# Gathering expert rows of two tables in alternation, and summing one of them wholly on the matrix engine

## The reference, cut to what matters

```python
def _peer(xn, wq, keys, u_tab, v_tab):
    q = (xt @ wq).reshape(t, PEER_HEADS, 2, PEER_HALF)
    sc = jnp.einsum('thkd,hknd->thkn', q, keys)
    s1, i1 = lax.top_k(sc[:, :, 0], 16); s2, i2 = lax.top_k(sc[:, :, 1], 16)
    ...                                   # best 16 of the 256 sums: experts, gates
    def block(args):                      # 128 tokens at a time
        ub = u_tab[eb]
        act = _gelu(jnp.einsum('td,thkd->thk', xb, ub)) * gb
        vb = v_tab[eb]
        return jnp.einsum('thk,thkd->td', act, vb)
```

## Time and profile before

| | |
|---|---|
| median of 3 runs | 3803.68 us (3803.42 to 3810.28) |
| profiled execution | 3807.15 us |
| its span, first to last instruction | 3805.4 us |
| busy: PE / DVE / POOL / ACT | 2685.4 / 2037.5 / 1864.6 / 802.3 us |
| granted PE clock, mean over the span | 0.850 |
| indirect transfers | 537 MB in 1024 rows |
| all transfers | 694 MB, mean 182 GB/s |

### The profile page before, as it was taken

How to read it: one execution, slowest core, us unless ns; L and a number is a source line. 1 busy time by engine, 2 the same in 40 slices (tenths; PEclk the granted TensorE clock), 3 DMA queues, 4 the chain that set the end, 5 groups by cost and what they waited for, 6 DMA issues and landing times.

```text
span 3805.4 us, 40545 instructions
## 1 busy us (share of the span) xinstructions
PE 2685.4 (71%) x15872; PEld 2087.4 (55%) x15872; DVE 2037.5 (54%) x4133; ACT 802.3 (21%) x1515; POOL 1864.6 (49%) x1389
## 2 busy tenths in 40 slices
PE   6521887207852287543767888888899998999999
PEld 4410444103431144211225777777789997789999
DVE  6589877888787878588444534454220103532010
ACT  2100111001110011111113322332332322433231
POOL 0166655775567756477752322221354543126463
PEclk7665998558986599766998988898899999999999
DMA  5398889997999879999981200000123332012332
GB/s 172 128 309 301 279 286 334 321 340 259 313 322 333 310 267 345 332 339 341 356 306 34 67 23 1 1 1 1 56 73 95 89 87 59 23 45 78 95 94 78
DMA packets 417984, 694.02 MB, mean 182 GB/s; under 512 B 35784, under 2 KB 280691, under 8 KB 417667
## 3 DMA queue, kind: packets, MB, share of 16 engines
q0 software_dynamic: 147456, 536.94, 39.7%
q1 hardware_dynamic: 270339, 154.50, 13.9%
HBM read 689.26 MB, written 2.10 MB: 182 GB/s over the span
## 4 chain that ended last, share of the span: by engine, by line
PE 51%; DVE 16%; POOL 13%; DMA 10%; issue 6%; ACT 3%; SPq 1%; DVEq 0%; ACTq 0%
PE PS L1593 25%; POOL ring L601 13%; DMA ring<-in_peer_v,eidx 7%; PE PS L768 6%; DMA ring<-in_peer_u,eidx 2%; PE PS L747 2%; DVE ring L1301 2%; PE PS L1495 1%; PE PS L1504 1%; PE PS L653 1%; PE PS L1501 1%; DVE X L1316 1%; PE PS L1603 1%; DVE W L1175 1%; PE PS L1615 1%
## 5 line engine op out<-in xcount | busy, mean ns | idle before, releaser
L601 POOL DMA_INDIRECT ring<-in_peer_u,eidx x512 | 635.8, 1242 | 404.0 <-DVE eidx L1278 177.9
L601 POOL DMA_INDIRECT ring<-in_peer_v,eidx x512 | 588.0, 1148 | 351.4 <-PE PS L768 192.1
L1593 PE MATMUL PS<-held_uH,GW 128*128 128x264 f32 (+1 forms) x3648 | 693.1, 290 | 35.9 <-POOL BIG_value L2120 31.8
L1301 DVE CUSTOM_DVE_ANT_0 ring<-ring,hn 128x1024 f32<-128x1024 f32 x512 | 614.7, 1223 | 115.6 <-DMA ring<-in_peer_u,eidx 106.8
L2106 POOL TENSOR_TENSOR GW<-held_wr,GW 128x1024 fp32r<-128x1024 f32 x178 | 428.6, 2409 | 453.2 <-ACT GW L1883 453.2
L768 PE MATMUL PS<-ring,dg 128*128 128x512 f32 x1024 | 528.2, 655 | 172.4 <-DMA ring<-in_peer_v,eidx 168.0
L1593 PEld LDWEIGHTS PS<-held_uH,GW 128*128 128x128 f32 x3648 | 581.7, 193 | 48.9 <-issue 32.4
L1593 PE MATMUL PS<-BIG_value,GW 128*128 128x264 f32 (+1 forms) x1824 | 486.1, 287 | 0.0
L768 PEld LDWEIGHTS PS<-ring,dg 128*128 128x128 f32 x1024 | 196.2, 206 | 460.6 <-DMA ring<-in_peer_v,eidx 276.6
L1316 DVE SCALAR_TENSOR_TENSOR X<-ring,gact,X 128x1024 f32<-128x1024 f32 x256 | 328.6, 1284 | 186.0 <-DMA ring<-in_peer_v,eidx 181.4
L1593 PE MATMUL PS<-hid,GW 128*128 128x264 f32 (+1 forms) x3072 | 370.4, 282 | 0.0
(11 more groups left out here) (465 smaller groups left out, 3613.2 us busy)
## 6 DMA issues: line engine op xcount, KB each, us to landing
held_wr<-in_w_ff SPq DMA_DIRECT2D x128, 512.0 KB, 4.0
wqr<-in_peer_wq SPq DMA_DIRECT2D x64, 512.0 KB
held_wr<-in_w_in_ab SPq DMA_DIRECT2D x18, 512.0 KB, 3.9
ring<-in_peer_u,eidx POOLq DMA_INDIRECT x512
ring<-in_peer_v,eidx POOLq DMA_INDIRECT x512
BIG<-in_w_in SPq DMA_DIRECT2D x4, 1536.0 KB, 11.4
held_wr<-in_w_qkv_c SPq DMA_DIRECT2D x12, 512.0 KB, 3.8
w_out<-in_w_out SPq DMA_DIRECT2D x1, 4096.0 KB, 19.0
```

Source lines behind the costliest of these rows:

```text
L601: e.indirect_dma_start(out=ring[:, i % RING, :], out_offset=None, in_=rows_u if k < HK else rows_v, in_offset=bass.IndirectOffsetOnAxis(ap ...
L1301: e.tensor_tensor_reduce(row, row, hn[:, :], 1.0, 0.0, ALU.mult, ALU.add, act[:, k:k + 1]).then_inc(*n.up(e_dot))
L1593: ins = e.matmul(bank[b + a][:, 0:w], w_[:, k * P:(k + 1) * P], x_[:, c0:c0 + w], start=(first and z in (0, 2)), stop=(last and z >= 4))
```

## The change

The new `first_order` keeps two counters, one of U rows and one of V rows. In block 0 the 128 U rows run as before, beside the front of block 0 only; then come 110 V rows of block 0 alone (HK - LAG), with all 76 steps of front 1 spread evenly over them. From then on each pass of the loop takes one U row of block 1, 2 or 3 and one V row, which lies 18 rows behind: V rows 110 to 127 of the block before, then 0 to 109 of the same block. In blocks 1 and 2 a step of the next front follows in two passes of three. In block 3 a step of the tails follows in one pass of four, until the first step of tail 2 is out. The last 18 V rows follow alone, then the end of block 3, and then what is left of the late steps: nine steps of tail 2, the projection for block 3, and tail 3.

All V rows go to PE; `expert_add` is gone, and every V row has a diagonal from ACT, up to three ahead. Gelu and the weighing are done for one head (16 columns) at a time. The ring has the same six slots, and its order follows the list.

```diff
+LAG = 18
...
-    def experts(blk, others, pace):
-        while heads(blk) < 1:
+    def add_u(others):
+        blk, k = divmod(count["u"], HK)
+        while heads(blk) < k // TOPK + 1:
             step(others)
-        order.append(("begin", blk))
-        if blk == NB - 1:
-            order.append(("second",))
-        for k in range(HK):
-            while heads(blk) < k // TOPK + 1:
-                step(others)
-            order.append(("u", blk, k))
-            if k % pace[0] == 0:
-                step(others)
-        while taken[("front", blk)] < FRONT_STEPS:
-            step(others)
-        order.append(("gate", blk))
-        for k in range(HK):
-            order.append(("v", blk, k))
-            if k % pace[1] == 0:
-                step(others)
-        order.append(("end", blk))
+        if k == 0:
+            order.append(("begin", blk))
+            if blk == NB - 1:
+                order.append(("second",))
+        order.append(("u", blk, k))
+        count["u"] += 1
+        if k % TOPK == TOPK - 1:
+            order.append(("gelu", blk, k // TOPK))
+        if ended:
+            order.append(("end", ended.pop()))
+    def add_v():
+        m = count["v"]
+        for x in range(m, min(m + NDG, NB * HK)):
+            blk, k = divmod(x, HK)
+            head = x // TOPK
+            if x in diagonals or count["u"] < TOPK * (head + 1) or taken[("front", blk)] < FRONT_STEPS:
+                continue
+            if head not in weighed:
+                order.append(("weigh", blk, k // TOPK))
+                weighed.add(head)
+            order.append(("dg", blk, k))
+            diagonals.add(x)
+        blk, k = divmod(m, HK)
+        order.append(("v", blk, k))
+        count["v"] += 1
+        if k == HK - 1:
+            ended.append(blk)
     fronts = [(("front", 0), FRONT_STEPS)]
     for _ in range(7):
...
-    while taken[("front", 0)] < 13:
+    for k in range(HK):
+        add_u(fronts)
+        if k % 3 == 0:
+            step(fronts)
+    while taken[("front", 0)] < FRONT_STEPS:
         step(fronts)
-    for blk, pace in ((0, (3, 2)), (1, (8, 2)), (2, (8, 2))):
-        fronts.append((("front", blk + 1), FRONT_STEPS))
-        experts(blk, fronts, pace)
-    while fronts:
-        step(fronts)
+    fronts.append((("front", 1), FRONT_STEPS))
+    for k in range(HK - LAG):
+        add_v()
+        while fronts and taken.get(("front", 1), 0) * (HK - LAG) < FRONT_STEPS * (k + 1):
+            step(fronts)
     late = []
     for b in range(3):
         late += [(("pproj", b), 1), (("tail", b), TAIL_STEPS)]
     late.append((("pproj", 3), 1))
-    experts(3, late, (4, 4))
+    for blk in range(1, NB):
+        for k in range(HK):
+            add_u(fronts)
+            if k == 0 and blk + 1 < NB:
+                fronts.append((("front", blk + 1), FRONT_STEPS))
+            add_v()
+            if blk == NB - 1:
+                if k % 4 == 3 and taken.get(("tail", 2), 0) < 1:
+                    step(late)
+            elif k % 3:
+                step(fronts)
+        while blk + 1 < NB and taken[("front", blk + 1)] < FRONT_STEPS:
+            step(fronts)
+    while count["v"] < NB * HK:
+        add_v()
+    order.append(("end", ended.pop()))
...
+    gathers = [name for name in first_order() if name[0] in ("u", "v")]
+    place = {name: i for i, name in enumerate(gathers)}
     def slot_free(e, i):
-        j = i - RING
-        if j < 0:
-            return
-        blk, k = j // 256, j % 256
-        if k < HK:
-            e.wait_ge(e_dot, HK * blk + k + 1)
-        elif k % 2:
-            e.wait_ge(e_pv, 64 * blk + (k - HK) // 2 + 1)
-        else:
-            e.wait_ge(e_ax, 64 * blk + (k - HK) // 2 + 1)
+        if i >= RING:
+            kind, blk, k = gathers[i - RING]
+            e.wait_ge(e_dot if kind == "u" else e_pv, HK * blk + k + 1)
     def first_pool(e):
-        for blk in range(NB):
-            for k in range(2 * HK):
-                i = 256 * blk + k
-                if k < HK and k % TOPK == 0:
-                    e.wait_ge(r_idx, NH * blk + k // TOPK + 1)
-                slot_free(e, i)
-                e.indirect_dma_start(
-                    out=ring[:, i % RING, :], out_offset=None, in_=rows_u if k < HK else rows_v,
-                    in_offset=bass.IndirectOffsetOnAxis(ap=eidx[:, blk % 2, k % HK:k % HK + 1], axis=0),
-                ).then_inc(d_r[i % RING], 16)
+        for i, (kind, blk, k) in enumerate(gathers):
+            if kind == "u" and k % TOPK == 0:
+                e.wait_ge(r_idx, NH * blk + k // TOPK + 1)
+            slot_free(e, i)
+            e.indirect_dma_start(
+                out=ring[:, i % RING, :], out_offset=None, in_=rows_u if kind == "u" else rows_v,
+                in_offset=bass.IndirectOffsetOnAxis(ap=eidx[:, blk % 2, k:k + 1], axis=0),
+            ).then_inc(d_r[i % RING], 16)
...
     def expert_sum(e, n, blk, k):
-        if k % 2:
-            i = k // 2
-            e.wait_ge(*row_there(256 * blk + HK + k))
-            e.wait_ge(e_dg, 64 * blk + i + 1)
-            for c in range(2):
-                ins = e.matmul(bank[6 + c], dg[:, i % NDG, :], ring[:, (256 * blk + HK + k) % RING, 512 * c:512 * c + 512],
-                               start=(k == 1), stop=(k == HK - 1))
-            ins.then_inc(*n.up(e_pv))
+        i, m = place["v", blk, k], HK * blk + k
+        e.wait_ge(*row_there(i))
+        e.wait_ge(e_dg, m + 1)
+        if k == 0 and blk:
+            e.wait_ge(e_x, blk)
+        for c in range(2):
+            ins = e.matmul(bank[6 + c], dg[:, m % NDG, :], ring[:, i % RING, 512 * c:512 * c + 512],
+                           start=(k == 0), stop=(k == HK - 1))
+        ins.then_inc(*n.up(e_pv))
...
-    def diagonal(e, n, blk, i):
-        if i < 64:
-            if i >= NDG:
-                e.wait_ge(e_pv, 64 * blk + i - NDG + 1)
-            e.mul(dg[:, i % NDG, :], ident, gact[:, 2 * i + 1:2 * i + 2]).then_inc(*n.up(e_dg))
-    def weigh_scalar(e, n, blk):
-        e.wait_ge(e_dot, HK * (blk + 1))
-        e.activation(gact[:, :], act[:, :], ACT.Gelu).then_inc(*n.up(e_gelu))
-        e.wait_ge(e_gact, blk + 1)
-        for i in range(NDG - 1):
-            diagonal(e, n, blk, i)
+    def diagonal(e, n, blk, k):
+        m = HK * blk + k
+        e.wait_ge(e_gact, m // TOPK + 1)
+        if m >= NDG:
+            e.wait_ge(e_pv, m - NDG + 1)
+        e.mul(dg[:, m % NDG, :], ident, gact[:, k:k + 1]).then_inc(*n.up(e_dg))
+    def gelu_scalar(e, n, blk, h):
+        at = slice(TOPK * h, TOPK * h + TOPK)
+        e.wait_ge(e_dot, HK * blk + TOPK * h + TOPK)
+        e.activation(gact[:, at], act[:, at], ACT.Gelu).then_inc(*n.up(e_gelu))
...
     def expert_dot(e, n, blk, k):
-        i = 256 * blk + k
+        i = place["u", blk, k]
         row = ring[:, i % RING, :]
         e.wait_ge(*row_there(i))
         if k == 0:
             e.wait_ge(e_hn, blk + 1)
         e.tensor_tensor_reduce(row, row, hn[:, :], 1.0, 0.0, ALU.mult, ALU.add, act[:, k:k + 1]).then_inc(*n.up(e_dot))
-    def weigh_vector(e, n, blk):
+    def weigh_vector(e, n, blk, h):
+        at = slice(TOPK * h, TOPK * h + TOPK)
         e.wait_ge(*n.next(e_gelu))
         e.wait_ge(r_gate, blk + 1)
-        e.tensor_tensor(gact[:, :], gact[:, :], gate[:, blk % 2, :], ALU.mult).then_inc(*n.up(e_gact))
+        e.tensor_tensor(gact[:, at], gact[:, at], gate[:, blk % 2, at], ALU.mult).then_inc(*n.up(e_gact))
         e.wait_ge(*n.now(e_gact))
-    def expert_add(e, n, blk, k):
-        if k % 2 == 0:
-            i = 256 * blk + HK + k
-            e.wait_ge(*row_there(i))
-            if k:
-                e.wait_ge(*n.now(e_ax))
-            e.scalar_tensor_tensor(X[:, blk, :], ring[:, i % RING, :], gact[:, k:k + 1], X[:, blk, :],
-                                   ALU.mult, ALU.add).then_inc(*n.up(e_ax))
     def experts_done(e, n, blk):
-        e.wait_ge(e_pv, 64 * (blk + 1))
-        e.wait_ge(*n.now(e_ax))
+        e.wait_ge(e_pv, HK * (blk + 1))
         for c in range(2):
             ins = e.tensor_tensor(X[:, blk, 512 * c:512 * c + 512], X[:, blk, 512 * c:512 * c + 512], bank[6 + c], ALU.add)
         ins.then_inc(*n.up(e_x))
```

More of the change, by code:

```diff
@@ L137, in first_order @@
     taken = {}
+    count = {"u": 0, "v": 0}
+    weighed = set()
+    diagonals = set()
+    ended = []
     def step(streams):
@@ L341, in emit @@
         "hs", "hTp", "hT", "q", "qT", "sc", "top", "idx", "ts", "gexp", "gate"))
-    e_hn, e_dot, e_gelu, e_gact, e_dg, e_pv, e_ax, e_x = (sem("e_" + x) for x in (
-        "hn", "dot", "gelu", "gact", "dg", "pv", "ax", "x"))
+    e_hn, e_dot, e_gelu, e_gact, e_dg, e_pv, e_x = (sem("e_" + x) for x in (
+        "hn", "dot", "gelu", "gact", "dg", "pv", "x"))
     t_xTp, t_xT, t_pTp, t_pT, t_pp, t_g, t_sig, t_gp, t_x, t_xn, t_hTp, t_hT, t_met = (sem("t_" + x) for x in (
@@ L995, in first_scalar @@
                 keep_hn(e, n, name[1])
-            elif name[0] == "gate":
-                weigh_scalar(e, n, name[1])
```

(13 more changed lines are left out.)

## The result

The changed kernel is slower: 3907.43 us (3894.72 to 3919.81) against 3804.76 us (the median of four runs); the ratio is 1.0258 with a 95% interval of 1.0231 to 1.0286. The profiled execution took 3897.87 us, its span is 3896.0 us, 90.7 us longer than the one of before. The medians lie 102.7 us apart; the two profiles show 90.7 us of that, and what follows accounts for those.

A forecast was written before the change was run, and what follows sets the result against it. It took the layer as already near its transfers' bound (DMA share 0.87 to 0.96). Rows ending 21 us later plus 30 us at the first block's end gave +51 us: 3855 us beside the 3803.7 median, likeliest range 3825 to 3890.

The forecast's parts named there:

- the wide one: Whole kernel: range of 3790 to 3910 us, taking in half of rival B, D and most of rival C.
- rival C: Blocks 1 and 2: stalls belong to steps, in-order queues hold rows, blocks stay at 456 us; 3915 us, chance 0.18.
- U phase of block 0: Block 0's 128 U rows beside the same front, bound by DVE: 232 us for 234, ending at 402 us.
- V rows alone: Block 0's 110 V rows with all of front 1: PE becomes the bound, 315 us, bounds 290 and 345.
- Blocks 1 and 2 in pairs: U and V rows alternating: transfers remain the longest, 426 us a block, a gain of 30 and 36; bounds 390 and 456.
- of the 26 us of stalls I keep 13: First 54 passes of blocks 1 and 2: 162 us of transfers plus 13 us of stalls, since steps are less dense.
- Block 3: Same 256 rows and 10 MB as before, when it took 407 us: 405 us, bounds 395 and 425.
- The last 18 V rows: V rows alone after block 3's pairs: PE 32 us, transfers 27, so 31 us.
- The tails: End of first block: tail 2's steps and block 3's projection join tail 3 behind the last row, +30 us, bounds 22 and 34.
- The new small waits: Added diagonals and Gelus: 0 us; waits for DVE's add to X at block ends: 3 us for three, bounds 0 and 10.
- The second block of the model: What runs after the first block's end: the forecast sum has no term for it.

The follow-up runs named there:

- e9: The kernel before, in its old order of phases, with every V row summed on PE through a diagonal; ratio 1.0381, 3970 us.
- e2: The changed kernel, but DVE adds every second of the 110 V rows that stand alone in block 0; ratio 1.0196, 3888 us.
- e6: The changed kernel with the 76 steps of the next front spread evenly over all 128 passes of blocks 1 and 2; ratio 1.0276.
- e7: The changed kernel with a front step in each pass of blocks 1 and 2 until none is left (76 passes); ratio 1.0260.
- e11: The kernel before with the next front's steps spread over both U and V phases of blocks 1 and 2, without alternation; ratio 0.9980.
- e3: The changed kernel with seven ring slots instead of six up to the end of block 2; ratio 1.0140, 3864 us.
- e4: The changed kernel with five ring slots in use instead of six throughout; ratio 1.0682, 4065 us.
- e10: The kernel before with seven ring slots up to the end of block 2; ratio 0.9837, 3766 us.
- e12: The kernel before with eight ring slots instead of six in block 3 only; ratio 0.9933, 3799 us.
- e5: The changed kernel, but in all four blocks DVE adds the even V rows and PE sums the odd ones; ratio 1.0335, 3943 us.

## Why the prediction came out as it did

The direction and both places named for the loss held; the size of +51 us was half of the +103 measured. The measured 3907 us lies outside the forecast's own range, 3825 to 3890, and 3 us inside the wide one, which reaches to 3910 only because most of rival C was taken into it. The terms, in their order:

- *U phase of block 0*: 401.9 against 402. Right.
- *V rows alone*: 296 us against 315, ending 19 us earlier than forecast. PE's work was 286 us where I had 294: the rows took 197 (195 forecast), the front 89 (99), at a granted clock of 0.99 against 0.91 in the phase of before; and I had kept 21 us of PE's idle where 9 were left. That PE bounds it is shown by the window and by e9. Freeing PE doesn't free the stretch (e2): a bound of 276 us lies right beneath.
- *Blocks 1 and 2 in pairs*: 451 and 457 us against 426. This step failed, and it is 56 us of the error. Cut by passes, top-k took 212 and 213 us for its 60 (I had 209) and the last 14 took 41 and 40 (42). The first 54 took 199 and 204 us against 175. The failed step is "of the 26 us of stalls I keep 13: a pass now carries two thirds of a step". At 350 GB/s these passes need 162 us, so 37 to 42 us of stalls stand there, more than the whole 26. e6, e7 and e11 show why thinning does not help: a stall goes with its step. e3, e4 and e10 show what it consists of: a round trip through six slots that is nearly filled by landing, use and reissue, so that little of a step's delay is covered. I had computed that stretch from bytes, and it is the number of slots that moves it. My rival C said just this, 456 us a block and 3915 us, and I gave it 0.18; its mechanism is what happened. That its 3915 came within 8 us of 3907 is partly luck: the other terms missed by -19, +16, +3, -3 and -5 us, and the second block of the model by -8.
- *Block 3*: 421 us against 405. I priced PE's wait for the late weights at nothing. PE did wait 21.8 us for them with V rows queued behind, and POOL up to 24.0 us for PE:

```profile
PE PS L810 <- DMA BIG<-in_meta_tokens: 21.8, 1, 21.8
```

  In these 22 us the transfers run at 395 GB/s, at a DMA share of 1.03, while DVE is busy 4 us and only two rows are issued. So how much of the 16 us is this wait and how much the 24 late steps with V rows behind them was not separated.
- *The last 18 V rows*: 34 us against 31.
- *The tails*: +24.6 us against +30, inside its bounds: the gate product ran in 14.0 us instead of 15.7, and tail 3's ACT and PE work began beside the projection.
- *The new small waits*: the Gelus and diagonals cost nothing that shows; ACT is busy 81 of 451 us in a block, and PE waited for DVE's add to X for 3.9 us, once in block 1, where I had priced 1 us for each of three.
- *The second block of the model*: priced at no change, it took 8 us less. The last section has what the profiles show of that.

The estimate from the Trainium skill's 358 GB/s (DMA: Bandwidth & Descriptors, Where 436 GB/s comes from), no block of pairs under 398 us, was never tested: the fastest block of pairs, e3's, took 431. Windows of 365 GB/s over 181 us (e12) and of 410 over 10 us lie above the figure, so no run here confirms it as a cap for this core.

## What to carry to other kernels

Where a ring of buffers feeds in-order engines, add up one slot's round trip (issue to landing, wait, use, reissue) before counting bytes or busy time: here 10.6 us over six slots was the pace. The sum says where a slot's time goes, and not what a slot more will win, since the round trip grows with the slots; a run with one slot more and one with one fewer tell that. A seventh slot was worth 20 us a block in either order, while thinning or packing the steps was worth nothing. Moving work off an engine that is 76% busy (DVE in block 0's V phase) onto another can make that one the bound of the stretch (PE, 286 of 295 us); a cut in one engine's work wins only down to the next bound, which can lie close beneath. Look also at what lands behind the last transfer when an order is rewritten: nine steps there cost 25 us, and putting them back among the rows cost nearly as much again.

## What the runs showed of the hardware that was not expected

With less work, PE ran slower. In e5 PE was busy 63% of block 1 and was granted 0.76 of its clock; in the changed kernel 78% and 0.96; a matmul of the V rows went from 645 to 891 ns.

The second block of the model is the same in all fourteen profiles and took 1776.8 to 1788.4 us in them. It took 1788 us in the five in which the clock stood at its lower level (1.2 GHz) for 235 to 239 us of it, and 1777 to 1781 us in the nine in which it did so for 203 to 221 us. The windows of the kernel before and of the changed kernel over that block:

```profile
2017.00:3805.40 1788.40, 1616.92 (x12297) 1510.24 (x12297) 540.03 (x1097) 555.97 (x1020) 640.56 (x361) 0.93 0.19 53
```

```profile
2116.00:3896.00 1780.00, 1609.05 (x12297) 1504.25 (x12297) 538.89 (x1097) 556.16 (x1020) 640.22 (x361) 0.94 0.19 53
```

The same instructions are 8 us apart. The longer time goes with the longer low clock in all fourteen, so a part of each difference between two single profiles here is likely the clock's.
